# Third mixer's tiles: the transposed inverse by VectorE's 32x32 transposes, and another deal of the background pieces

## Chip, cores, metric

One core of a Trainium2 chip runs the whole program as one launch. The metric is the device time in microseconds, the median of three runs. All data is float32. TensorE takes the big products as three products of a high part and a remainder.

## The reference, cut to what matters

One layer of a hybrid decoder: RMSNorm, one input projection, four token mixers in parallel (HGRN2, RWKV-7, GLA, mLSTM), merge gates, an output projection, and an MLP with squared ReLU. 1040 prompt tokens (16 learned, 1024 given) and 8 sequences of 4 sample tokens share the weights. The change touches the RWKV-7 mixer, called here the third mixer, since the kernel runs it third. For each of its 4 heads (64 keys, 64 values), token by token:

```python
sa = jnp.einsum('bhvk,bhk->bhv', s, kkt)
s = (s * jnp.exp(lwt)[:, :, None, :] - sa[..., None] * (kkt * at)[:, :, None, :]
     + vt[..., None] * kt[:, :, None, :])
return s, jnp.einsum('bhvk,bhk->bhv', s, rt)
```

## The kernel before, in words

**Tiles.** The 1072 tokens are columns, padded to three groups of 358. The mixers run one after another: mLSTM, then HGRN2 and GLA together (the second mixer's loop), then RWKV-7. Each takes tiles of 128 tokens, 8 of them, and a ninth of 48 tokens, in which the last prompt tokens and the samples stand and masks keep the sequences apart. Within a tile RWKV-7's recurrence is solved in closed form: a strictly triangular 128x128 matrix A per head, of scores between the tokens' removal keys, gives the triangular inverse of (I - A), by which the right-hand side is multiplied; state and output follow.

**The inverse.** It is built by doubling. Level 0 puts the scores next to the diagonal into an identity matrix (blocks of 2). Level l, for l = 1 to 6 with halves of 2, 4, ... 64, joins pairs of blocks: it takes A times the first halves of the inverse, then the second halves' inverse times that. Two copies are kept, T in tile RTT (`tt`) and its transpose in RTI (`ti`), because a product on TensorE takes one operand transposed. The four heads stand side by side in 512 columns. A level is:

1. TensorE, L1226: four products of 64 columns (eight instructions in the trace) of A with `ti`, into a bank. They wait for `ti` of the level before.
2. ScalarE, L1644: copies them to RM1 (`m1`).
3. TensorE, L1234: `m1` with `tt`, which gives the new part of `ti` (not at the last level), and L1238: the same two the other way round, which gives the new part of `tt`.
4. VectorE, L2306 in `select`: puts the new part into `ti`, then into `tt`, under a mask, each after its product.

Besides, each tile has on TensorE at its head the scores (L1216 to L1218; L1218 gives those for `ti`), after level 1 the transposes of the output of the tile before (L1181), after level 2 the transposes of keys and values (L1246, L1248), after level 4 the right-hand side (L1200, L1192), the same lines again after level 6 for the output, the solution (L1259), the output (L1266) and the new state (L1284, L1285). VectorE masks the scores (`masked`, L2280), selects level 0 into `ti` (L2275) and into `tt` (L2287), and updates the state (L2354, L2359), for which the next tile's head waits (semaphore rw_pre).

**Background pieces.** While the mixers wait for other engines, TensorE works at the input projection of what comes later (here the merge gates). `fill_work` is a generator; one `steps(gate, k)` puts k pieces into TensorE's program at that place. A piece is three products of 358 columns (L442). Eight pieces fill one of two banks, 48 make one pair of weight chunks, and each pair of tiles consumes 48, so 24 to a tile. ScalarE empties the banks (`steps(outs, 1)`, three times a tile, one of them after level 4) and takes the high part of the next weights; GpSimd subtracts it to get the remainder.

**Order.** It is written out by hand. Each engine runs its own program in order and meets the others by counting semaphores. `rw_t` counts VectorE's results in a tile, `rw_n` the products of L1234 and L1238 that are ready, `rw_m` and `rw_m1` those of L1226 and the copies. `rw_ti`, `rw_tt` and the constants RW_PER_T, RW_PER_N say which count belongs to which level. The loop over tiles is a hardware loop over pairs, with the first pair and the ninth tile written apart. No planner is involved.

Of the kernel before, what the change touches and what calls it, by code (L numbers as in the profile page):

```python
# [26 lines left out]
HALVES = [1, 2, 4, 8, 16, 32, 64]  # L27
LHALVES = [1, 2, 4, 8]
# [109 lines left out]
def build(nc, A, OUT, fcols, ucols, fdim, udim):  # L138
    ctx = ExitStack()
    with ctx:  # L140
# [12 lines left out]
        def S(name):  # L153
            return sems[name]
# [12 lines left out]
        def PS(b, lo=0, hi=512):  # L167
            return PSt[:, b * 512 + lo:b * 512 + hi]
# [21 lines left out]
        def mask8(name, k, rows=P):  # L190
            o, n = ucols[name]
            w = {"lv": P, "lvt": P, "ll": LASTW, "llt": LASTW}[name]
            return CU[0:rows, o + k * w:o + (k + 1) * w]
# [33 lines left out]
        def half(x, h, second):  # L227

            names = " ".join("abc"[:len(x.shape) - 2])
            y = x.rearrange(f"p {names} (n t) -> p {names} n t", t=2 * h)  # L230
            return y[(slice(None),) * (len(y.shape) - 1) + (slice(h, 2 * h) if second else slice(0, h),)]
# [4 lines left out]
        def bc(x, shape):  # L236
            return x.to_broadcast(shape)
# [278 lines left out]
        def steps(work, k):  # L516
            for _ in range(k):
                next(work, None)
# [93 lines left out]
        Q_GL, Q_RW, Q_GATE, Q_END = 2, 7, 11, 27  # L612
        Q_GL_TILES, Q_GL_TAIL, Q_RW_PRE, Q_RW_TILES, Q_RW_TAIL = 9, 17, 18, 21, 25

        def rw_ti(l):
            return 1 if l == 0 else 3 if l == 1 else 2 * l + 2

        def rw_tt(l, last):
            return 2 if l == 0 else 4 if l == 1 else 2 * l + 2 if last else 2 * l + 3
        RW_PK, RW_PER_T, RW_PER_N = 5, 2 * len(HALVES), 2 * len(HALVES) - 3  # L620

# [293 lines left out]
        def _(e):  # L917
# [5 lines left out]
            for k in range(KD):  # L923
                e.wait_ge(S("ht_ready"), k + 1)
                for g in range(3):
                    last = e.matmul(PS(3 + g, 0, GRP)[0:68], WS[:, k, :], XT[:, k, g * GRP:(g + 1) * GRP],  # L926
                                    start=k == 0, stop=k == KD - 1)
# [3 lines left out]
                for g in range(3):  # L931
                    last = three(e, PS(g, 0, GRP), 0, k, slice(g * GRP, (g + 1) * GRP), k == 0, k == KD - 1)
# [12 lines left out]
            for t in range(TILES + 1):  # L945
                w = P if t < TILES else LASTW
                for u in range(2):
                    o = t * 2 * P + u * P
                    last = e.transpose(PSt[0:w, o:o + P], VT[:, u, t * P:t * P + w], ident)
# [4 lines left out]
            for q, src in enumerate((RSC, RKH)):  # L954
                for g in range(3):
                    last = e.matmul(PS(3 * q + g, 0, GRP), const("sel4", 4), src[:, g * GRP:(g + 1) * GRP],
                                    start=True, stop=True)
            last.then_inc(S("ml_bc"), 1)
            for t in range(TILES + 1):
                w = P if t < TILES else LASTW  # L960
                last = e.transpose(PS(0, GRP, 512)[0:w, 4 * t:4 * t + 4], RM[:, t * P:t * P + w], ident[0:4, 0:4])
# [67 lines left out]
            for g in range(3):  # L1029
                last = e.matmul(PS(g, 0, GRP), WGA[0:16, :], GA[0:16, g * GRP:(g + 1) * GRP], start=True, stop=True)  # L1030
# [139 lines left out]
            def rw_tile(n, w, last_tile, gate, rc, first=False):  # L1170
                levels = LHALVES if last_tile else HALVES
                nlev = len(levels)
# [39 lines left out]
                for h in range(4):  # L1212
                    r, g = slice(64 * (h % 2), 64 * (h % 2) + 64), h // 2

                    ab = rc[r, g:g + 3:2, 0:w]
                    e.matmul(PS(h % 2, g * 2 * w, (g + 1) * 2 * w)[0:w], rc[r, 6 + g, 0:w], ab, start=True, stop=True)  # L1216
                    e.matmul(PS(2 + h % 2, g * 2 * w, (g + 1) * 2 * w)[0:w], rc[r, 4 + g, 0:w], ab, start=True, stop=True)
                    last = e.matmul(PS(4 + h % 2, g * w, g * w + w)[0:w], rc[r, g, 0:w], rc[r, 6 + g, 0:w], start=True, stop=True)  # L1218
                last.then_inc(S("rw_s"), 1)
                steps(gate, 8 if last_tile else 7)  # L1220
                for l in range(1, nlev):

                    lh, m = levels[l], w // 2
                    e.wait_ge(S("rw_t"), t0 + (2 if l == 1 else rw_ti(l - 1)))
                    for h in range(4):
                        last = e.matmul(PS(4, h * m, h * m + m)[0:w], pb[0:w, 2 * h * w:2 * h * w + w],  # L1226
                                        half(ti[0:w, h * w:h * w + w], lh, False), start=True, stop=True)
                    last.then_inc(S("rw_m"), 1)
                    steps(gate, 6 if last_tile else 1)
                    e.wait_ge(S("rw_m1"), n * 6 + l)  # L1230
                    e.wait_ge(S("rw_t"), t0 + rw_tt(l - 1, False))
                    if l < nlev - 1:
                        for h in range(4):
                            last = e.matmul(PS(1, h * m, h * m + m)[0:w], tt[0:w, h * w:h * w + w],  # L1234
                                            half(m1[0:w, h * w:h * w + w], lh, False), start=True, stop=True)
                        last.then_inc(S("rw_n"), 1)
                    for h in range(4):
                        last = e.matmul(PS(0, h * m, h * m + m)[0:w], m1[0:w, h * w:h * w + w],  # L1238
                                        half(tt[0:w, h * w:h * w + w], lh, True), start=True, stop=True)
                    last.then_inc(S("rw_n"), 1)  # L1240
                    if l == 1 and not first:
                        back_to_rows(n - 1, P)
                    if l == 2:
                        e.wait_ge(S("rw_t"), t0 + RW_PK)
                        for j in range(4):
                            e.transpose(PS(2, j * P, j * P + P)[0:w], rc[:, 4 + j, 0:w], ident)  # L1246
                        for j in range(2):
                            last = e.transpose(PS(3, j * P, j * P + P)[0:w], rc[:, 8 + j, 0:w], ident)  # L1248
                        last.then_inc(S("rw_kt"), 1)
                    if l == 4:  # L1250
                        rhs()
# [2 lines left out]
                keys(1, 1)  # L1254
                seen(1, 1, False)
                e.wait_ge(S("rw_r"), n + 1)
                e.wait_ge(S("rw_t"), t0 + rw_tt(nlev - 1, True))
                for h in range(4):
                    last = e.matmul(PS(5, h * 64, h * 64 + 64)[0:w], tt[0:w, h * w:h * w + w], RRS[0:w, h * 64:h * 64 + 64],  # L1259
                                    start=True, stop=True)  # L1260
# [21 lines left out]
                else:  # L1282
# [2 lines left out]
                        last = e.matmul(PS(0, g * P, g * P + P), RKB[:, 256 + g * P:256 + g * P + P], RUS[:, g * P:g * P + P],  # L1285
                                        start=False, stop=True)
                    last.then_inc(S("rw_ds"), 1)
                steps(gate, 24 if last_tile else 9)
                if last_tile:
                    back_to_rows(n, w)  # L1290

# [472 lines left out]
        def _(e):  # L1764
# [3 lines left out]
            for i in range(KD // 2):  # L1768
                e.wait_ge(S("norm_sq"), 2 * i + 2)
                j = (2 * i) % 4  # L1770
# [457 lines left out]
            def rw_tile(n, w, last_tile, first=False):  # L2228
# [27 lines left out]
                if not last_tile:  # L2256
# [2 lines left out]
                        ec = REC[:, g, bass.ds(n, 1)]  # L2259
                        ins = e.tensor_scalar(RXC[:, g * P:g * P + P], RST0[:, g * P:g * P + P], ec, None, ALU.mult)  # L2260
                    st.did(ins)
                e.tensor_copy(ti, bc(idw.unsqueeze(1), [w, 4, w]))
                st.did(e.tensor_copy(tt, bc(idw.unsqueeze(1), [w, 4, w])))
                if not first:
                    r = [RMS_[:, k] for k in range(4)]
# [5 lines left out]

                mk = bc(mask8("ll" if last_tile else "lv", 0, w).unsqueeze(1), [w, 2, w])
                mkt = bc(mask8("llt" if last_tile else "lvt", 0, w).unsqueeze(1), [w, 2, w])
                for j in range(2):
                    ins = e.copy_predicated(ti[:, j:4:2, :], mkt, PS(4 + j, 0, 2 * w)[0:w].rearrange("p (h t) -> p h t", h=2))  # L2275
                ins.then_inc(S("rw_t"), 1)
                def masked(dst, bank):
                    for j in range(2):
                        out = dst.rearrange("p (i j c) -> p i j c", i=2, j=2)[:, :, j, :]
                        ins = e.tensor_tensor(out, PS(bank + j, 0, 4 * w)[0:w].rearrange("p (i c) -> p i c", i=2),  # L2280
                                              bc(cm.unsqueeze(1), [w, 2, 2 * w]), ALU.mult)
                    return ins
                masked(pb, 0)

                for j in range(2):
                    src = PS(j, 0, 4 * w)[0:w].rearrange("p (i k t) -> p i k t", i=2, k=2)[:, :, 0, :]
                    ins = e.copy_predicated(tt[:, j:4:2, :], mk, src)  # L2287
                ins.then_inc(S("rw_t"), 1)
                if last_tile:
                    e.wait_ge(S("states_in"), (11 + 8 + 4) * 16)  # L2290
                    e.wait_ge(S("rw_pre"), n + 1)
# [10 lines left out]
                def select(dst, bank, mk, ready):  # L2302
                    e.wait_ge(S("rw_t"), t0 + at)
                    e.wait_ge(S("rw_n"), n0 + ready)
                    e.sem_inc(S("select_turn"), 1)
                    e.copy_predicated(dst, bc(mk.unsqueeze(1), dst.shape),  # L2306
                                      PS(bank, 0, 2 * w)[0:w].rearrange("p (a n t) -> p a n t", a=4, t=h)).then_inc(S("rw_t"), 1)
                for l, h in list(enumerate(levels))[1:]:
                    if l < nlev - 1:
                        select(half(ti, h, False), 1, half(mask8("llt" if last_tile else "lvt", l, w), h, False), 2 * l - 1)  # L2310
                        at += 1
                    select(half(tt, h, True), 0, half(mask8("ll" if last_tile else "lv", l, w), h, True), 2 * l - (l == nlev - 1))
                    at += 1
                    if l == 1:
                        masked(pk, 2).then_inc(S("rw_t"), 1)
                        at += 1
                        if not first:
                            output(n - 1, P)
# [274 lines left out]
```

## Time and profile before

| | |
|---|---|
| median of 3 runs | 2424.34 us (2422.03 to 2425.43) |
| profiled execution | 2420.86 us, its span 2419.1 us |
| mean granted clock of TensorE | 0.958 |
| TensorE busy | 2215.7 us (92%) |
| VectorE busy | 1046.7 us (43%) |
| ScalarE busy | 609.4 us (25%) |
| GpSimd busy | 457.2 us (19%) |
| the 8 full tiles of the third mixer | from some 967 to 1275 us |

The span is the time from the first to the last instruction. PE is TensorE, PEld its loading of weights, which overlaps products, DVE VectorE, ACT ScalarE, POOL GpSimd, SP SyncE. L1226 is line 1226 of the kernel. PEclk is the granted clock of TensorE, 1.00 for 2.4 GHz and 0.50 for 1.2 GHz. In a timeline, "x8" are eight instructions merged, the time is from the first start to the last end, and the brackets give idle time before it and what ended it. The chain is followed back from the last instruction, and its pieces begin where the piece before ended. Ends of products are modelled.

### The profile page before, as it was taken

What the parts mean: (1) busy time and instruction counts of PE and PEld (TensorE: products, weight loads), DVE (VectorE), ACT (ScalarE), POOL (GpSimd) and SP (SyncE); (2) the same over time, 40 slices, a digit from 0 to 9 for tenths busy, and PEclk for the clock granted to TensorE, in tenths of its full rate; (3) what the DMA queues carried; (4) which work ended last, traced back from release to release, by engine and by line L of the source; (5) the groups of instructions that cost most, each with busy time, mean ns of one, the idle gap of its engine ahead of it and who ended that gap; (6) DMA issues with size and microseconds to landing.
All of it is one profiled execution on the core that took longest, in us unless ns stands there. A gap on an engine that the chain in (4) does not pass through costs nothing.

```text
span 2419.1 us, 33549 instructions
## 1 busy us (share of the span) xinstructions
PE 2215.7 (92%) x13459; PEld 2094.0 (87%) x13459; DVE 1046.7 (43%) x1568; ACT 609.4 (25%) x801; POOL 457.2 (19%) x463
## 2 busy tenths in 40 slices
PE   5989998899999888999998699999999979999995
PEld 3978787799899776999998689999999979999994
DVE  4142331565655545333333266642222225655554
ACT  3422221432322143212121143011000013333342
POOL 1131113344443421010000266110000010000012
PEclk9999998999999888999998799999999989999997
DMA  4121124222222231010101465131111233111112
GB/s 149 44 68 54 53 62 123 95 62 67 70 71 69 83 127 54 19 46 18 36 18 36 142 225 194 44 113 47 43 43 43 80 121 140 41 37 43 43 43 81
DMA packets 48562, 178.39 MB, mean 74 GB/s; under 512 B 6400, under 2 KB 6752, under 8 KB 48240
## 3 DMA queue, kind: packets, MB, share of 16 engines
q1 hardware_dynamic: 23040, 85.72, 11.7%
q0 software_dynamic: 17648, 62.03, 7.4%
q10 hardware_dynamic: 7808, 29.71, 3.2%
q8 instruction: 48, 0.79, 0.1%
q14 instruction: 18, 0.15, 0.0%
HBM read 129.41 MB, written 48.02 MB: 73 GB/s over the span
## 4 chain that ended last, share of the span: by engine, by line
PE 80%; DVE 6%; ACT 4%; issue 3%; DMA 3%; PEld 1%; POOL 1%; PEldq 0%; DVEq 0%; POOLq 0%; SPq 0%; ACTq 0%
PE PS L442 23%; PE PS L599 20%; PE PS L1355 15%; PE PS L1316 4%; PE PS L1059 2%; PE PS L1238 2%; PE PS L1234 2%; PE PS L1226 2%; DMA RING<-in_w_all 1%; PE PS L1071 1%; PEld PS L442 1%; PE PS L1192 1%; PE PS L926 1%; DVE AR L1979 1%; PE PS L1200 1%
## 5 line engine op out<-in xcount | busy, mean ns | idle before, releaser
L442 PE MATMUL PS<-HT_parts,WHIA_parts 128*128 128x358 f32 x1440 | 516.6, 359 | 37.1 <-POOL RING_parts L437 18.6
L442 PE MATMUL PS<-OT_parts,WHIA_parts 128*128 128x358 f32 x1440 | 482.1, 335 | 0.0
L442 PE MATMUL PS<-HT_parts,RING_parts 128*128 128x358 f32 x1440 | 480.1, 333 | 0.0
L1355 PE MATMUL PS<-ACT_parts,CF_parts 128*128 128x358 f32 x1152 | 319.0, 331 | 24.6 <-DVE ACT_parts L577 13.8
L442 PEld LDWEIGHTS PS<-HT_parts,WHIA_parts 128*128 128x128 f32 x1440 | 281.5, 195 | 58.1 <-POOL RING_parts L437 20.3
L437 POOL TENSOR_TENSOR RING_parts<-RING,WHIA_parts 128x1024 fp32r<-128x1024 f32 x60 | 154.0, 2566 | 856.3 <-ACT WHIA_parts L432 856.3
L442 PEld LDWEIGHTS PS<-OT_parts,WHIA_parts 128*128 128x128 f32 x1440 | 281.6, 196 | 3.6
L442 PEld LDWEIGHTS PS<-HT_parts,RING_parts 128*128 128x128 f32 x1440 | 280.6, 195 | 0.0
L599 PE MATMUL PS<-HT_parts,CF_parts 128*128 128x358 f32 x768 | 251.7, 328 | 0.9 <-ACT AR L566 0.9
L599 PE MATMUL PS<-OT_parts,CF_parts 128*128 128x358 f32 x768 | 251.2, 327 | 0.0
L599 PE MATMUL PS<-HT_parts,RING_parts 128*128 128x358 f32 x768 | 250.8, 327 | 0.0
L1355 PE MATMUL PS<-ACT_parts,RING_parts 128*128 128x358 f32 x768 | 250.3, 326 | 0.0
L1355 PEld LDWEIGHTS PS<-ACT_parts,CF_parts 128*128 128x128 f32 x1152 | 206.9, 189 | 33.9 <-issue 28.4
L1733 ACT ACTIVATE ACT_parts<-AR 128x1074 fp32r<-128x1074 f32 x96 | 105.8, 1103 | 192.9 <-PE PS L1355 178.5
L599 PEld LDWEIGHTS PS<-HT_parts,CF_parts 128*128 128x128 f32 x768 | 144.6, 188 | 1.3 <-ACT AR L566 1.2
L599 PEld LDWEIGHTS PS<-OT_parts,CF_parts 128*128 128x128 f32 x768 | 145.2, 189 | 0.1
L599 PEld LDWEIGHTS PS<-HT_parts,RING_parts 128*128 128x128 f32 x768 | 144.9, 189 | 0.0
L1355 PEld LDWEIGHTS PS<-ACT_parts,RING_parts 128*128 128x128 f32 x768 | 144.6, 188 | 0.0
L477 ACT ACTIVATE AR<-PS 128x358 f32<-128x358 f32 x102 | 47.6, 467 | 348.9 <-PE PS L442 348.8
L2444 DVE SCALAR_TENSOR_TENSOR AR<-PS,AR 128x1074 f32 (+1 forms) x32 | 40.8, 1276 | 208.5 <-PE PS L599 201.9
L1355 PE MATMUL PS<-CF_parts 128*128 128x358 f32 x384 | 125.2, 326 | 0.0
L551 POOL TENSOR_TENSOR AR<-AR 128x1074 f32<-128x1074 f32 x14 | 33.9, 2423 | 460.4 <-ACT AR L544 460.4
(392 smaller groups left out, 3523.7 us busy)
## 6 DMA issues: line engine op xcount, KB each, us to landing
RING<-in_w_all SPq DMA_DIRECT2D x132, 512.0 KB, 3.3
AR<-gates POOLq DMA_DIRECT2D x32, 537.0 KB, 4.0
proj<-AR ACTq DMA_DIRECT2D x18, 537.0 KB, 5.1
AR<-proj POOLq DMA_DIRECT2D x18, 537.0 KB, 8.6
gates<-CF ACTq DMA_DIRECT2D x16, 537.0 KB, 5.2
gates<-AR ACTq DMA_DIRECT2D x16, 537.0 KB, 5.3
AR<-in_xT SPq DMA_DIRECT2D x8, 537.0 KB, 14.4
AR<-in_xT POOLq DMA_DIRECT2D x8, 537.0 KB, 6.8
```

The costliest lines, as they stand in the source:

```text
L437: e.tensor_tensor(RING_R[:, u], RING[:, u], WHIA_R[:, u].bitcast(F32), ALU.subtract).then_inc(S(f"split{u}"), 1)
L442: last = e.matmul(out, a_[:, u, k, :], b_[:, k, t], start=first and i == 0, stop=end and i == 2)
L477: e.activation(row[:, g * GRP:(g + 1) * GRP], PS(6 + c % 2, 0, GRP), ACT.Copy).then_inc(S("fill_free"), 1)
L599: last = e.matmul(PS(3 * u + g, 0, GRP), a_[:, u, k, :], b_[:, k, t], start=k == 0 and i == 0, stop=k == KD - 1 and i == 2)
L1059: last = e.matmul(PS(3 * (l % 2), lo * m, hi * m)[0:w], x[:, g, l, 0:w], GQB[:, l % 2, lo * m:hi * m], start=True, stop=True)
L1226: last = e.matmul(PS(4, h * m, h * m + m)[0:w], pb[0:w, 2 * h * w:2 * h * w + w], half(ti[0:w, h * w:h * w + w], lh, False), start=True, s ...
L1234: last = e.matmul(PS(1, h * m, h * m + m)[0:w], tt[0:w, h * w:h * w + w], half(m1[0:w, h * w:h * w + w], lh, False), start=True, stop=True)
L1238: last = e.matmul(PS(0, h * m, h * m + m)[0:w], m1[0:w, h * w:h * w + w], half(tt[0:w, h * w:h * w + w], lh, True), start=True, stop=True)
L1316: last = e.matmul(PS(3 * u + tg, 0, GRP), a_[:, v, k, :], b_[:, k, t], start=k == 2 * br and i == 0, stop=k == 2 * br + 1 and i == 2)
L1355: last = e.matmul(PS(3 * v + g, 0, GRP), a_[:, u, 4 * v + r % 4, :], b_[b][:, t], start=r == 0 and i == 0, stop=r == 31 and i == 2)
L1733: e.activation(AHI_R[r % 2], act_row(r), ACT.Copy).then_inc(S("act_hi"), 1)
L2444: e.scalar_tensor_tensor(row3(dst), cols3(3 * u), 0.0, row3(RST2), ALU.max, ALU.mult).then_inc(S(f"banks_free{u}"), 1)
```

## The change

In the eight full tiles `ti` is no longer built by products up to level 4, that is up to blocks of 32. VectorE transposes all of `tt` in 32x32 blocks into `ti` (`flip`, 128x512 elements in one instruction) at level 0 and after the select of `tt` at levels 1 to 4. Since `tt` then holds nothing outside its blocks of 32, this is its transpose. L1218, L1234 of levels 1 to 4, L2262, L2275 and the selects into `ti` of levels 1 to 4 go. At levels 5 and 6, and in the ninth tile, all stays. VectorE now selects level 0 into `tt` before the masking, and the transpose stands behind it. L1226 waits for the transpose of the level before. The counts are renumbered. The pieces of a tile are dealt out otherwise: 5 after the scores (7 before), 3 between L1226 and the next product at levels 1 to 4 (1 before), 1 at levels 5 and 6 as before, 2 after L1259 as before, 3 at the end (9 before).

```diff
-                    last = e.matmul(PS(4 + h % 2, g * w, g * w + w)[0:w], rc[r, g, 0:w], rc[r, 6 + g, 0:w], start=True, stop=True)
+                    if last_tile:
+                        last = e.matmul(PS(4 + h % 2, g * w, g * w + w)[0:w], rc[r, g, 0:w], rc[r, 6 + g, 0:w], start=True, stop=True)
                 last.then_inc(S("rw_s"), 1)
-                steps(gate, 8 if last_tile else 7)
+                steps(gate, 8 if last_tile else 5)
...
-                    steps(gate, 6 if last_tile else 1)
+                    steps(gate, 6 if last_tile else 3 if l <= RW_FLIPS else 1)
                     e.wait_ge(S("rw_m1"), n * 6 + l)
-                    e.wait_ge(S("rw_t"), t0 + rw_tt(l - 1, False))
-                    if l < nlev - 1:
+                    e.wait_ge(S("rw_t"), t0 + rw_tt(l - 1, last_tile))
+                    if l < nlev - 1 and (last_tile or l > RW_FLIPS):
...
-                steps(gate, 24 if last_tile else 9)
+                steps(gate, 24 if last_tile else 3)
...
+                def flip(at):
+
+                    e.wait_ge(S("rw_t"), t0 + at)
+                    e.transpose(flat[0], flat[1]).then_inc(S("rw_t"), 1)
+                if last_tile:
+                    masked(pb, 0)
+                    first_level()
+                else:
+                    first_level()
+                    masked(pb, 0)
+                    flip(1)
...
+                    flips = not last_tile and l <= RW_FLIPS
+                    if l < nlev - 1 and not flips:
+                        select(half(ti, h, False), 1, half(mask8("llt" if last_tile else "lvt", l, w), h, False), rw_n(l, last_tile, False))
                         at += 1
...
+                    if flips:
+                        flip(at)
+                        at += 1
```

## Rows read from the trace of the kernel before

**Rows 1.** Page, chain that ended last: share of the span by engine.
```profile
PE 80%; DVE 6%; ACT 4%; issue 3%; DMA 3%; PEld 1%; POOL 1%; PEldq 0%; DVEq 0%; POOLq 0%; SPq 0%; ACTq 0%
```

**Rows 2.** Stretches of one third-mixer tile: engines' busy us, granted clock, DMA.
```profile
core 0: us, PE busy (x) PEld busy (x) DVE busy (x) ACT busy (x) POOL busy (x), PEclk, DMA share, GB/s
...
1044.70:1082.99 38.29, 37.90 (x288) 35.67 (x289) 13.96 (x36) 7.95 (x19) 2.36 (x1) 1.00 0.10 29
```

**Rows 3.** Chain in that tile, in order of time: start us, us, what.
```profile
1044.72 0.67 PE PS L1216 x2
...
1047.66 3.65 PE PS L442 x21
...
1052.16 0.55 PE PS L442 x3
1052.71 1.05 PE PS L1234 x8
1053.75 0.89 PE PS L1238 x8
1054.65 0.22 PE PS L1181 x2
...
1058.34 0.44 PE PS L1246 x4
1058.79 0.22 PE PS L1248 x2
...
1061.49 0.89 PE PS L1238 x8
1062.38 0.89 PE PS L1226 x8
...
1065.83 0.89 PE PS L1200 x8
1066.72 0.50 PE PS L1192 x4
...
1078.20 4.44 PE PS L442 x27
```

**Rows 4.** Groups of VectorE's instructions, 880 to 1300 us: busy us, mean ns.
```profile
L2280 DVE TENSOR_TENSOR AR<-PS,CF 128x512 f32<-128x512 f32 x32 | 20.6, 686 | 0.0
...
L2158 DVE SCALAR_TENSOR_TENSOR AR<-AR,CC 128x1039 f32<-128x1039 f32 x4 | 5.2, 1293 | 0.0
...
L2263 DVE COPY AR<-CF 128x512 f32<-128x512 f32 x8 | 3.3, 419 | 0.0
```

**Rows 5.** VectorE in that tile, in order of time: start us, us, instruction.
```profile
1047.92 0.78 DVE L2275 COPY_PREDICATED AR<-CU,PS 128x256 f32<-128x256 uint8 x2 [4.94 <-PE PS L1218]
...
1049.79 0.77 DVE L2287 COPY_PREDICATED AR<-CU,PS 128x256 f32<-128x256 uint8 x2
...
1054.87 0.73 DVE L2306 COPY_PREDICATED AR<-CU,PS 128x256 f32<-128x256 uint8 x1 [0.23 <-PE PS L1238]
...
1062.54 0.43 DVE L2306 COPY_PREDICATED AR<-CU,PS 128x256 f32<-128x256 uint8 x1 [0.46 <-PE PS L1238]
...
1079.04 0.61 DVE L2359 SCALAR_TENSOR_TENSOR AR<-AR 128x128 f32<-128x128 f32 x2
```

**Rows 6.** TensorE in that tile, in order of time.
```profile
1062.22 1.06 PE L1226 MATMUL PS<-AR 128*128 128x64 f32 x8
```

**Rows 7.** Stretches with and without the full clock, columns as in rows 2.
```profile
487.14:527.46 40.32, 39.41 (x243) 37.32 (x242) 23.04 (x53) 10.81 (x17) 16.30 (x24) 0.96 0.20 59
527.46:566.34 38.88, 37.97 (x243) 35.76 (x242) 23.17 (x53) 10.72 (x17) 17.43 (x24) 1.00 0.20 62
...
909.54:911.83 2.29, 0.33 (x2) 0.03 (x1) 2.29 (x3) 0.00 (x0) 0.00 (x0) 1.00 0.00 0
...
913.20:926.80 13.60, 13.49 (x34) 9.56 (x33) 3.20 (x3) 5.59 (x5) 0.00 (x0) 0.50 0.00 1
1312.60:1336.40 23.80, 20.84 (x88) 20.33 (x89) 10.04 (x27) 1.42 (x2) 1.08 (x1) 0.50 0.00 1
```

More of the change, by code:

```diff
@@ L613, in build, with rw_ti, rw_tt, rw_n @@
         Q_GL_TILES, Q_GL_TAIL, Q_RW_PRE, Q_RW_TILES, Q_RW_TAIL = 9, 17, 18, 21, 25
[L615 to L620, printed above, removed]
+        def rw_ti(l, last_tile):
+            if last_tile:
+                return 1 if l == 0 else 3 if l == 1 else 2 * l + 2
+            return 2 if l == 0 else 4 if l == 1 else 2 * l + 3 if l <= RW_FLIPS else 2 * l + 2
+        def rw_tt(l, last_tile):
+            nlev = len(LHALVES if last_tile else HALVES)
+            if last_tile:
+                return 2 if l == 0 else 4 if l == 1 else 2 * l + 2 if l == nlev - 1 else 2 * l + 3
+            return 1 if l == 0 else 3 if l == 1 else 2 * l + 2 if l <= RW_FLIPS or l == nlev - 1 else 2 * l + 3
+        def rw_n(l, last_tile, second):
+            flips = 0 if last_tile else RW_FLIPS
+            if l <= flips:
+                return l
+            nlev = len(LHALVES if last_tile else HALVES)
+            return flips + 2 * (l - flips) - (1 if l == nlev - 1 or not second else 0)
+        RW_FLIPS = 4
+        RW_PK, RW_PER_T, RW_PER_N = 5, 2 * len(HALVES), 2 * len(HALVES) - 3 - RW_FLIPS
         @block.sync
@@ L1216, in rw_tile @@
                     e.matmul(PS(h % 2, g * 2 * w, (g + 1) * 2 * w)[0:w], rc[r, 6 + g, 0:w], ab, start=True, stop=True)
-                    e.matmul(PS(2 + h % 2, g * 2 * w, (g + 1) * 2 * w)[0:w], rc[r, 4 + g, 0:w], ab, start=True, stop=True)
-                    last = e.matmul(PS(4 + h % 2, g * w, g * w + w)[0:w], rc[r, g, 0:w], rc[r, 6 + g, 0:w], start=True, stop=True)
+                    last = e.matmul(PS(2 + h % 2, g * 2 * w, (g + 1) * 2 * w)[0:w], rc[r, 4 + g, 0:w], ab, start=True, stop=True)
+                    if last_tile:
+                        last = e.matmul(PS(4 + h % 2, g * w, g * w + w)[0:w], rc[r, g, 0:w], rc[r, 6 + g, 0:w], start=True, stop=True)
                 last.then_inc(S("rw_s"), 1)
-                steps(gate, 8 if last_tile else 7)
+                steps(gate, 8 if last_tile else 5)
                 for l in range(1, nlev):
                     lh, m = levels[l], w // 2
-                    e.wait_ge(S("rw_t"), t0 + (2 if l == 1 else rw_ti(l - 1)))
+                    e.wait_ge(S("rw_t"), t0 + (2 if l == 1 else rw_ti(l - 1, last_tile)))
                     for h in range(4):
@@ L1256, in rw_tile @@
                 e.wait_ge(S("rw_r"), n + 1)
-                e.wait_ge(S("rw_t"), t0 + rw_tt(nlev - 1, True))
+                e.wait_ge(S("rw_t"), t0 + rw_tt(nlev - 1, last_tile))
                 for h in range(4):
@@ L2261, in rw_tile @@
                     st.did(ins)
-                e.tensor_copy(ti, bc(idw.unsqueeze(1), [w, 4, w]))
+                if last_tile:
+                    e.tensor_copy(ti, bc(idw.unsqueeze(1), [w, 4, w]))
                 st.did(e.tensor_copy(tt, bc(idw.unsqueeze(1), [w, 4, w])))
@@ L2273, in rw_tile @@
                 mkt = bc(mask8("llt" if last_tile else "lvt", 0, w).unsqueeze(1), [w, 2, w])
-                for j in range(2):
-                    ins = e.copy_predicated(ti[:, j:4:2, :], mkt, PS(4 + j, 0, 2 * w)[0:w].rearrange("p (h t) -> p h t", h=2))
-                ins.then_inc(S("rw_t"), 1)
+                if last_tile:
+                    for j in range(2):
+                        ins = e.copy_predicated(ti[:, j:4:2, :], mkt, PS(4 + j, 0, 2 * w)[0:w].rearrange("p (h t) -> p h t", h=2))
+                    ins.then_inc(S("rw_t"), 1)
                 def masked(dst, bank):
@@ L2282, in masked, with first_level @@
                     return ins
[L2283 to L2288, printed above, removed]
+                def first_level():
+                    for j in range(2):
+                        src = PS(j, 0, 4 * w)[0:w].rearrange("p (i k t) -> p i k t", i=2, k=2)[:, :, 0, :]
+                        ins = e.copy_predicated(tt[:, j:4:2, :], mk, src)
+                    ins.then_inc(S("rw_t"), 1)
+                def flip(at):
+                    e.wait_ge(S("rw_t"), t0 + at)
+                    e.transpose(flat[0], flat[1]).then_inc(S("rw_t"), 1)
+                if last_tile:
+                    masked(pb, 0)
[4 more added lines that the diff above has]
+                    flip(1)
                 if last_tile:
@@ L2308, in rw_tile @@
                 for l, h in list(enumerate(levels))[1:]:
-                    if l < nlev - 1:
-                        select(half(ti, h, False), 1, half(mask8("llt" if last_tile else "lvt", l, w), h, False), 2 * l - 1)
+                    flips = not last_tile and l <= RW_FLIPS
+                    if l < nlev - 1 and not flips:
+                        select(half(ti, h, False), 1, half(mask8("llt" if last_tile else "lvt", l, w), h, False), rw_n(l, last_tile, False))
                         at += 1
-                    select(half(tt, h, True), 0, half(mask8("ll" if last_tile else "lv", l, w), h, True), 2 * l - (l == nlev - 1))
+                    select(half(tt, h, True), 0, half(mask8("ll" if last_tile else "lv", l, w), h, True), rw_n(l, last_tile, True))
                     at += 1
+                    if flips:
+                        flip(at)
+                        at += 1
                     if l == 1:
```

## The prediction

> **What bounds the kernel now.** The chain that ended last is read first: TensorE products hold 80% of it [rows 1]. Then the table of stretches, one row for each third-mixer tile: the tile from 1044.70 to 1082.99 us lasts 38.29 us, TensorE shows work for 37.90 of them and its granted clock is 1.00, its upper level, 2.4 GHz [rows 2]. VectorE is busy for 13.96 us and ScalarE for 7.95 us. Last the chain inside that tile, in order of time [rows 3]: products follow each other without a hole, because each wait for VectorE is covered by products that TensorE still has to issue, and each wait for ScalarE by one piece of the background projection. So what is taken from TensorE's list in these tiles is a gain, as long as it does not uncover a wait. There are 8 such tiles; the short ninth keeps its old way.
>
> **What the change removes from TensorE.** Each number is for one tile.
> - L1218, the transposed first-level scores: 8 of the 24 passes that run from 1044.72 to 1047.66 [rows 3]. 2.94 / 24 = 0.12 us each, so 0.98 us.
> - L1234, the product for the transposed inverse, at levels 1 to 4. Before, one piece (0.55 us) and L1234 (1.05 us, part of it waiting for ScalarE's copy) stand between L1226 and L1238, together 1.60 us at level 1; the other three levels repeat this at 1.64 to 1.65 [rows 3]. The piece is kept, at 0.52 (21 matmuls, seven pieces, in 3.65 us [rows 3]). So 1.08 + 1.13 + 1.12 + 1.13 = 4.46 us go. That the copy stays hidden follows: three pieces, 1.56 us, now stand where 0.55 us of piece and a short wait stood.
> Removed: 5.44 us. The 24 pieces per tile are only dealt out anew (5 + 4x3 + 2x1 + 2 + 3 in place of 7 + 6x1 + 2 + 9), so they cost the same.
>
> **What it adds.** The transposed block is now a copy of the block that L1238 has just given: select, then a transpose of 128x512 elements on VectorE (call its time F), then the next L1226. Between L1238 and that L1226 TensorE has no piece: all three stand after L1226. Before, L1234's result was selected while L1238 ran, which hid it. TensorE issues in order, so the pieces behind L1226 wait too.
>
> The trace before has no transpose on VectorE. The nearest rows are 0.42 us for a plain copy of 128x512 (L2263), 0.69 us for a product of 128x512 with a PSUM source (L2280) and 1.29 us for 128x1039 (L2158), as if each element went through twice [rows 4]. I take 0.69: the same number of elements, and the copy's faster pace needs no reordering across lanes. The ends are kept for the range. No gain below zero is possible: the transpose is a new instruction in a chain of dependent ones.
>
> At level 3, L1238 ends at 62.38; the select runs from 62.54 for 0.43 [rows 5], to 62.97; the transpose to 63.66; 0.15 for the wake-up (as L1238 to select) gives 63.81. TensorE would have gone on at 62.38, and L1226 also loses an overlap of 0.17 with its predecessor (1.06 alone [rows 6] against 0.89 in the chain [rows 3]). Stall: 1.43 + 0.17 = 1.60 us. The other levels differ by what TensorE still has behind L1238:
> - level 1: the select takes 0.73 from 54.87 [rows 5], so 55.60 + 0.69 + 0.15 = 56.44, against 54.87 when L1181 ends: 1.57 + 0.17 = 1.74.
> - level 2: L1246 and L1248 cover 0.66: 0.94.
> - level 4: L1200 and L1192 cover 1.39: 0.21.
> Sum over levels: 1.74 + 0.94 + 1.60 + 0.21 = 4.49 us.
>
> At the head five pieces end at 47.66 + 2.60 = 50.26. VectorE's two selects and two masks take until about 49.79, as before but in the other order [rows 5]; with the transpose and the wake-up 50.63: 0.37 + 0.17 = 0.54. At the tail three pieces, 3 x 0.49 (27 in 4.44 [rows 3]), end at 79.68; the state update L2359 ends at 79.65 [rows 5], plus 0.15 = 79.80: 0.12 + 0.17 = 0.29. Nine pieces covered it before. The copy L2262 (0.42, as L2263 [rows 4]) and the two selects L2275 (0.78) that leave VectorE free it before the next tile, where it waits anyway: nothing. Behind the transpose of level 1 VectorE has the masked key products (2 x 0.69 [rows 4]) and the output of the tile before; level 2's three pieces and two products (1.56 + 2 x 0.89) run meanwhile, so they are covered. The background bank's evacuation by ScalarE falls due earlier in the tile, two pieces after the copy of level 4 behind which it is issued; ScalarE is busy for a fifth of the tile [rows 2], so nothing is put down. Without that cover TensorE would wait some tenths once a tile, 0.8 us in all for each tenth.
>
> Added: 4.49 + 0.54 + 0.29 = 5.32 us. Net at an unchanged clock: 5.32 - 5.44 = -0.12 us a tile, -1 us over 8. With F = 0.42 each of four transposes gives back 0.27 and level 4 its 0.21: -10 us more, so -11. With F = 1.29 five grow by 0.60: +24, so +23.
>
> A rule bears on F. By the Trainium skill, "VectorE: DVE Perf Modes", section "The three transpose paths", the engine transposes 128x128 in bf16 in 311 ns; four times that, an estimate from the page without any fixed part shared, is 1.24 us, and the sum would be +21 us. No transpose in the rows can settle it.
>
> **The clock.** This term decides. Today these tiles stand at 1.00. The rows show where it falls [rows 7]. From 909.54 to 911.83 TensorE worked for only 0.33 us, and from 913.20 the clock was at 0.50, its lower level, 1.2 GHz, for 13.60 us. In a tile of the second mixer, the stretch from 487.14, a drop came with TensorE busy for 39.41 of 40.32 us: the mean is 0.96, and the next tile, with the same work, stays at 1.00. And it doesn't come back by being busy: from 1312.60 to 1336.40 TensorE was busy for 20.84 of 23.80 us, mostly with the ninth tile's thin state products, and stayed at 0.50. The new tile puts, twice (after levels 1 and 3), products of 64 columns for 0.9 us, a hole of 1.4 to 1.6 us, and again 0.9 us of them, with no piece between. The hole is a little shorter than the one at 909.54; the work on both sides of it is thinner than a piece, whose products have 358 columns. The level 2 and level 4 places are filled by transposes and right sides.
>
> Price: the tile at 0.96 takes 40.32 against 38.88, 1.44 us more, and 0.04 x 2 x 40.32 = 3.2 us of it were at half: 0.45 us for each us at half. How often and for how long is an estimate. Of 16 such places I let 6 drop the clock, in six different tiles: of the two tiles of the second mixer one fell. A low stretch lasts between 3.2 (second mixer) and 23.8 us; 11 is taken, since the five pieces of the next head are the first solid work after level 4. 6 x 11 x 0.45 = 30 us. Bounds: 0, and 8 x 23.8 x 0.45 = 86 us.
>
> The same is said by the Trainium skill, "TensorE: Matmul & The Clock Gate", section "A second HAM failure mode: psum-queue depth-cycling": short idles between groups of products make the clock swing between its two rates. It speaks against this change, and the rows agree with it.
>
> **Sum.** -1 + 30 = +29 us. The profiled execution took 2420.86 us (span 2419.1 and 1.8 around it), 3.5 below the median of the runs, 2424.34. From the median: 2453 us. Faster or slower means by over 0.2%, 4.9 us, about what a measurement tells from no change.
>
> **Rivals.**
> - The clock holds and the transposes are short. Place: the hole behind L1238, levels 1 and 3. Price: F = 0.42 gives -11 us, 2413. For it: before, 24 thin products a level at 1.00 with one piece never cost the clock, and each hole is under 2 us. Against: those had no hole at all. It decides below F of about 0.6, if the clock stays at 1.00.
> - The clock holds, F near 0.69: the products go and as long waits come, 2423. For it: every step's size is read from rows. Against: the clock rows.
> - The clock falls in every tile and stays low until the next head: 8 x 20 x 0.45 = 72 us, 2495. For it: the stretch to 1336.40. Against: three pieces a level are solid work in between.
> - Transposes go at the slow pace with the clock holding: +23, 2447.
>
> **Chances.** Forecast (the clock falls in some tiles) 0.52, all tiles 0.12, slow transposes with the clock holding 0.05, clock holds and no change 0.18, clock holds and short transposes 0.13. Of the first, few falls may leave it near zero. So slower 0.68, same 0.18, faster 0.14. Range 2417 to 2488: from the clock-holds cases to most of the every-tile case; the forecast alone, two to eleven drops at 5 us each, has 2433 to 2478.
>
> **What would show it.** The tile's stretch in the table: clock below 1.00 in several of the eight, lengths unequal, some near 38 us and some over 42. TensorE idle behind L1238 at levels 1 and 3 by 1.4 to 1.6 us, at level 4 under 0.3, released by VectorE's transpose; a transpose row near 0.69 us. L1234 at a third of its count, L1218 only in the ninth tile. It is wrong if all eight stand at 1.00, or if TensorE's holes are under 1 us.

## Result and profile after

The changed kernel takes 2436.82 us (median of 6 runs, 2429.98 to 2450.85) against 2423.40 for the kernel before beside it (6 runs, 2422.03 to 2425.46): 13.4 us more, a ratio of 1.006 [1.0031, 1.0089]. A second series of 12 runs gave 1.0049 [1.0032, 1.0067]. It is slower, within the forecast's range, and by less than half of what was forecast. The profiled execution took 2435.24 us (span 2433.7) at a mean granted clock of 0.954, where the one before took 2420.86 us at 0.958. L1226 is now L1240, L1234 is L1248, L1238 is L1252, L1181 is L1194, L1200 is L1213, L1259 is L1273, L2306 is L2334, and the new transpose is L2309.

The page's chain by engine is that of [rows 1] within a per cent; it doesn't tell the two kernels apart.

```profile
PE 81%; DVE 6%; ACT 4%; issue 3%; DMA 3%; POOL 1%; PEldq 0%; POOLq 0%; DVEq 0%; PEld 0%; SPq 0%; ACTq 0%
```

The stretches do. Each row is one third-mixer tile of the changed kernel, and the last lies inside one; columns as in rows 2.

```profile
1008.32:1049.01 40.69, 36.64 (x249) 34.46 (x249) 14.44 (x34) 8.06 (x19) 7.10 (x6) 0.92 0.12 40
1049.01:1089.54 40.53, 36.79 (x249) 34.48 (x249) 14.64 (x35) 7.87 (x19) 2.35 (x1) 0.92 0.08 28
1089.54:1127.77 38.23, 33.74 (x249) 31.33 (x249) 14.91 (x37) 8.31 (x20) 2.36 (x1) 1.00 0.08 29
...
1061.20:1064.50 3.30, 3.30 (x17) 3.30 (x16) 0.71 (x3) 0.00 (x0) 0.00 (x0) 0.50 0.00 0
```

TensorE has 40 matmuls fewer in a tile than in [rows 2] (249 for 289, by the count of weight loads: L1218 and four levels of L1248), and in the tile with the full clock it works 33.74 us in place of 37.90. That tile is hardly shorter than before all the same (38.23 us; the same tile took 38.66). The tiles ahead of it stand at 0.92 and last 2.3 to 2.5 us longer, with the same work. The last row lies in one of the drops, as stretches at half clock are called here: the clock is at its lower level, 1.2 GHz, and TensorE is busy throughout. All eight tiles, from head to head:

| tile | 0 | 1 | 2 | 3 | 4 | 5 | 6 | 7 | sum |
|---|---|---|---|---|---|---|---|---|---|
| before, us | 39.94 | 38.03 | 38.27 | 38.66 | 38.26 | 38.65 | 38.26 | 38.40 | 308.5 |
| after, us | 40.86 | 40.69 | 40.53 | 38.23 | 40.73 | 40.90 | 37.83 | 40.88 | 320.6 |
| us at half clock, before | 4.4 | 0 | 0 | 0 | 0 | 0 | 0 | 0 | 4.4 |
| us at half clock, after | 8.3 | 6.8 | 6.8 | 0 | 6.8 | 6.8 | 0 | 6.8 | 42.3 |

So 12.2 of the 14.6 us between the two spans lie in these tiles. Of the other 2.4 us, 0.7 lie ahead of the first tile's head and 1.7 behind the eighth tile; they were not followed to a line.

What fills a tile that keeps the clock is seen in its chain of waits (start us, us, what), the tile from 1089.54, level 1 and the start of level 2. It answers to [rows 3].

```profile
1093.82 0.63 DVE AR L2309
...
1094.49 1.10 PE PS L1240 x8
1095.59 1.54 PE PS L442 x9
1097.14 0.85 PE PS L1252 x8
...
1098.12 0.73 DVE AR L2334
...
1098.88 0.72 DVE AR L2309
...
1099.65 1.10 PE PS L1240 x8
```

L1248 is gone from levels 1 to 4. The three pieces stand where one piece and L1234 stood, and behind L1252 the chain passes over to VectorE, to the select and the transpose, before the next level can start. TensorE's own order shows these waits in brackets: idle time before a group, here called a hole, and what ended it, at levels 2 and 4 (behind L1252 of levels 1 and 3).

```profile
1099.65 1.10 PE L1240 MATMUL PS<-AR 128*128 128x64 f32 x8 [1.45 <-DVE AR L2309]
...
1109.36 1.10 PE L1240 MATMUL PS<-AR 128*128 128x64 f32 x8 [1.37 <-DVE AR L2309]
```

VectorE's group for the transpose, over the stage (columns as in rows 4), gives its price:

```profile
L2309 DVE STREAM_TRANSPOSE AR<-AR 128x512 f32<-128x512 f32 x40 | 28.4, 710 | 1.1
```

The chain in the tile from 1049.01, behind its second drop, shows where the clock goes back up:

```profile
1070.03 1.10 PE PS L1240 x8
1071.13 2.51 PE PS L442 x9
1073.64 1.43 PE PS L1252 x8
1075.07 0.89 PE PS L1213 x8
```

The drop begins at 1071.3, with level 4's three pieces, which take 2.51 us where 1.54 is their time at the full clock. It ends at 1074.7, within L1252, and the next group is back at 0.89, as at the full clock. All 11 new drops of this execution last 3.4 us, two in each of five tiles and one in the first, each behind a hole of 1.4 us.

### The profile page after: what moved, and what is told of

The parts are those of the page before. It is cut to its first block, busy times and chain, and to the rows that moved or that the text cites. A ratio compares the mean times of both kernels' runs of the same rounds, so it can differ in the third digit from the quotient of the medians.

```text
span 2433.7 us, 32840 instructions
## 1 busy us (share of the span) xinstructions
PE 2192.4 (90%) x13139; PEld 2071.3 (85%) x13139; DVE 1049.5 (43%) x1552; ACT 609.0 (25%) x801; POOL 469.5 (19%) x463
## 4 chain that ended last, share of the span: by engine, by line
PE 81%; DVE 6%; ACT 4%; issue 3%; DMA 3%; POOL 1%; PEldq 0%; POOLq 0%; DVEq 0%; PEld 0%; SPq 0%; ACTq 0%
PE PS L442 25%; PE PS L599 19%; PE PS L1369 15%; PE PS L1330 4%; PE PS L1240 2%; PE PS L1072 2%; PE PS L1252 2%; DVE AR L2309 1%; PE PS L1084 1%; DMA RING<-in_w_all 1%; PE PS L939 1%; PE PS L1205 1%; PE PS L1107 1%; PE PS L1213 1%; PE PS L1100 1%
## 5 line engine op out<-in xcount | busy, mean ns | idle before, releaser
L437 POOL TENSOR_TENSOR RING_parts<-RING,WHIA_parts 128x1024 fp32r<-128x1024 f32 x60 | 163.0, 2716 | 870.8 <-ACT WHIA_parts L432 870.8
```

Source lines behind the costliest of these rows:

```text
L437: e.tensor_tensor(RING_R[:, u], RING[:, u], WHIA_R[:, u].bitcast(F32), ALU.subtract).then_inc(S(f"split{u}"), 1)
```

## Experiments

In what follows thin products are those of 64 columns, solid ones the pieces' of 358, and the deal is how a tile's 24 pieces are spread over it. Theory 1: the products removed and the waits added weigh about the same, and the slowdown is the clock, which falls at the holes behind L1252. Theory 2: the waits alone do it, and the clock's drops are small beside them. The ratios are against the kernel before, run on the same chip in turn: 2425.56 us for the first four kernels, 2427.27 for the next four, 2427.64 for the last two.

**Discarded products in the holes.** Ten products of 256 columns, whose result is never read, stand behind L1252 of levels 1 and 3. They fill most of the holes of 1.4 us (0.27 and 0.15 us are left, still ended by the transpose) and take nothing away.

```diff
+                    if not last_tile and l in (1, 3):
+                        for _ in range(10):
+                            e.matmul(PS(4, 256, 512), HT_R[:, 0, 0:P], HT_R[:, 0, 0:256], start=True, stop=True)
```

> The change, and ten products of 256 columns (some 1.2 us, their result is never read) behind L1252 at levels 1 and 3 of each full tile, shorter than the holes there (1.4 to 1.6 us), so that no wait gets longer. Theory 1, the clock: the change loses 2.7 us in each of six tiles because the clock drops for 3.4 us twice in them, and drops because those two holes leave TensorE too little to do. Then all eight tiles stand at 1.00 and take 37.8 to 38.3 us, and the whole is 16 us under the change: 2420 us, 0.998 of before. Theory 2, the waits: the holes themselves cost the time and the clock is a bystander. Then filling them with useless work brings nothing: 2437, or later.

Measured: 2421.22 us (2416.11 to 2427.16), ratio 0.9993 [0.9981, 1.0004]. One tile's stretch (columns as in rows 2); the other tiles are like it, the first at 0.95 as before the change:

```profile
1083.70:1121.91 38.21, 36.12 (x268) 33.70 (x269) 14.94 (x37) 8.30 (x20) 2.35 (x1) 1.00 0.08 29
```

TensorE works 2.4 us more than in the tile of 38.23 us above (36.12 against 33.74), in the same length, and the kernel takes 0.9993 of the time before where the changed one takes 1.006. Theory 2 falls: with the same waits for VectorE the kernel takes no longer than the kernel before, once TensorE works through them. Theory 1 holds.

**Pieces behind L1252.** The same holes, filled with work that is needed: level 1 and 3 have one piece behind L1240 and three behind L1252, levels 2 and 4 one and one.

```diff
-                    steps(gate, 6 if last_tile else 3 if l <= RW_FLIPS else 1)
+                    steps(gate, 6 if last_tile else {1: 1, 2: 1, 3: 1, 4: 1}.get(l, 1))
...
+                    if not last_tile:
+                        steps(gate, {1: 3, 2: 1, 3: 3, 4: 1}.get(l, 0))
```

> The change with its pieces in another place: behind L1226 one piece at each level, and behind L1252 (the product whose result is transposed) 3, 1, 3, 1 at levels 1 to 4; head 5, tail 3, as in the change. Theory 1: the holes are filled by useful work, so the clock stays at 1.00 and the wait for the transpose is hidden; by the rows of before, 38.3 less 5.4 removed, plus 0.6 (the wait for ScalarE's copy is back), 0.85 left of the holes and 0.8 at head and tail = 35.2 us a tile, 25 us under before: 2398, 0.990. Theory 2 (the chain of VectorE sets the tile, wherever the pieces stand): 38 us a tile, 2420 to 2437.

Measured: 2400.74 us (2398.18 to 2410.57), ratio 0.99 [0.9884, 0.9917]; tiles of 34.86 to 35.52 us at 1.00, but for the first (36.45 us at 0.93). A tile, and the chain at level 1 (in the tile before it):

```profile
1085.97:1121.49 35.52, 34.36 (x248) 31.05 (x249) 14.94 (x37) 8.28 (x20) 2.35 (x1) 1.00 0.09 31
```

```profile
1057.43 1.10 PE PS L1252 x8
1058.53 1.53 PE PS L442 x9
1060.07 0.22 PE PS L1194 x2
1060.28 1.04 PE PS L1240 x8
```

From L1252 to the next L1240 the chain stays on TensorE: VectorE's select and transpose are hidden under the pieces. A tile is 3.1 us shorter than before (38.66 to 35.52 for the one shown), 25 us over eight. So the transposes do bring a gain when the pieces stand behind the products that they wait for.

**The old deal with the transposes.** 7 pieces at the head, 1 a level, 9 at the tail, all else as changed.

```diff
-                steps(gate, 8 if last_tile else 5)
+                steps(gate, 8 if last_tile else 7)
...
-                    steps(gate, 6 if last_tile else 3 if l <= RW_FLIPS else 1)
+                    steps(gate, 6 if last_tile else 1)
...
-                steps(gate, 24 if last_tile else 3)
+                steps(gate, 24 if last_tile else 9)
```

> The change with the pieces dealt as before (7 at the head, 1 a level, 9 at the end): the transposes alone. Theory 1: the same holes with two pieces less a level around them, so the clock drops more often and stays down longer, 10 to 20 us a tile: 2450 to 2480 us. Theory 2 (the loss comes from the new deal, that is from the waits it uncovers at head and tail): those waits are covered again, 4.7 removed against 4.5 of holes a tile: 2421 us, the clock aside.

Measured: 2542.15 us (2527.49 to 2555.85), ratio 1.0483 [1.0465, 1.05]. The direction is theory 1's; the size is missed by 60 us, since I had each drop last too short. A tile, and the chain of waits in the tile before it:

```profile
1085.56:1140.11 54.55, 51.26 (x248) 49.49 (x249) 14.61 (x34) 8.06 (x19) 2.36 (x1) 0.62 0.07 20
```

```profile
1040.76 1.97 PE PS L1240 x8
1042.73 1.00 PE PS L442 x3
1043.73 1.61 PE PS L1252 x8
...
1079.69 5.41 PE PS L442 x27
```

Its tiles last 54.4 to 55.0 us, but for the first of 56.70 and one of 47.18. 41 us of the 54.55 are at half clock (0.38 x 2 x 54.55), and each group takes up to twice its time (L1252 1.61 against 0.85, a piece 1.00 against 0.52). One piece a level doesn't bring the clock back; it rises in the nine pieces of the tail, but in the tile of 47.18 us already in the two pieces behind L1273. Against the 38.39 us of the same tile with the clock held (the old deal with discarded products, below) that is 16.2 us for 41 us at half clock, 0.40 for each.

**The new deal without the transposes.** The kernel before with 5, 3 a level up to level 4, and 3.

```diff
-                steps(gate, 8 if last_tile else 7)
+                steps(gate, 8 if last_tile else 5)
...
-                    steps(gate, 6 if last_tile else 1)
+                    steps(gate, 6 if last_tile else 3 if l <= 4 else 1)
...
-                steps(gate, 24 if last_tile else 9)
+                steps(gate, 24 if last_tile else 3)
```

> The kernel before with only the new deal of the pieces (5, 3 at levels 1 to 4, 1 at levels 5 and 6, 2, 3), no transposes. Theory 1: no hole arises, the clock stays at 1.00 in all tiles; the wait for ScalarE's copy goes (0.6 us a tile) and waits at head and tail come (0.8): within 4 us of before, 2419 to 2427. Theory 2 (the deal itself costs, by ScalarE's evacuations falling due too early or by the tail's cover): 10 us or more over before, 2433.

Measured: 2420.23 us (2416.24 to 2427.64), ratio 0.9985 [0.997, 1.0]. A tile:

```profile
1082.39:1120.62 38.23, 37.20 (x289) 35.67 (x289) 14.41 (x39) 8.28 (x20) 2.35 (x1) 1.00 0.08 29
```

The deal alone doesn't lower the clock: no hole over 0.3 us stands among its thin products. The two parts of the change don't add. The deal alone is worth about -4 us (its interval -7 to 0), the transposes alone +117, both together +13: the deal is what keeps the transposes' drops short.

**Discarded products at level 1 only, and at level 3 only.** Which of the two holes costs?

```diff
-                    if not last_tile and l in (1, 3):
+                    if not last_tile and l in (1,):
```

> The change with the ten discarded products behind L1252 at level 1 alone; the hole of level 3 stays open. Theory 1a, each hole drops the clock by itself: one drop of 3.4 us stays in most tiles, 1.35 us each, so some 8 us over the run with both holes filled (2421): 2428 to 2431 us. Theory 1b, the first drop brings on the second (the tile is late and thin after it): with level 1 filled both go, and the time is that of the run with both filled, 2421 us.

Measured: 2446.24 us (2438.76 to 2452.59), ratio 1.0077 [1.0051, 1.0103]. Both expectations were below it. There were fewer drops (three new ones in the profiled execution), but one of them lasted 27.3 us. Its tile and the one behind it, and the chain from level 4 to the next head:

```profile
1053.89:1103.73 49.84, 46.92 (x258) 45.31 (x259) 15.68 (x38) 8.66 (x21) 2.35 (x1) 0.73 0.07 23
1103.73:1141.95 38.22, 34.88 (x259) 32.53 (x259) 13.98 (x34) 7.64 (x18) 2.35 (x1) 1.00 0.10 29
```

```profile
1074.83 2.10 PE PS L442 x9
1076.92 1.60 PE PS L1252 x8
1078.52 1.71 PE PS L1213 x8
...
1082.79 1.00 PE PS L442 x3
...
1095.67 1.90 PE PS L442 x6
...
1100.98 2.40 PE PS L442 x9
```

The clock fell at 1075.6, when part of level 4's pieces had already gone. What was left of them didn't bring it back, nor did the single pieces of levels 5 and 6 (1.00) and the two behind the solution (1.90); it rose in the three of the tail, after 27.3 us. Two pieces at that place are not always too few: in the old deal's tile of 47.18 us the clock rose in them, after 20.5 us, and the next group is back at 0.84.

```profile
1343.35 1.66 PE PS L442 x6
1345.01 0.84 PE PS L1280 x8
```

The same hole, then, costs 1.4 us (3.4 x 0.40) or 11.6 (49.84 - 38.22), by how much solid work is still to come behind the fall, and when. That is a reading of where the drops ended; no run here varied the moment of the fall by itself.

The other one:

```diff
-                    if not last_tile and l in (1, 3):
+                    if not last_tile and l in (3,):
```

> The mirror image: the ten discarded products behind L1252 at level 3 alone; the hole of level 1 stays open. With level 1 filled (2446 us) fewer tiles dropped, but one drop, behind level 3, lasted 27 us: after level 4 there is no solid work before the next head. Theory: what a drop costs depends on the pieces that follow it. A drop at level 1 is followed by three levels of three pieces, so each lasts 3.4 us (some 6.8): up to 1.4 us in each of eight tiles, on the 2421 of both holes filled: 2422 to 2433 us, no stretch over 10 us. Rival: the length is a matter of chance or of the hole's size alone (level 1's is the longer one): as with level 1 filled, 2440 or more.

Measured: 2426.75 us (2423.22 to 2430.34), ratio 0.9997 [0.9987, 1.0007]. In the profiled execution a single tile dropped once, for 3.4 us:

```profile
1163.82:1203.46 39.64, 36.52 (x259) 34.06 (x259) 14.88 (x37) 8.30 (x20) 2.36 (x1) 0.96 0.08 27
```

So the hole behind level 3 is the costly one, and with it filled the one behind level 1, open in all eight tiles, is nearly harmless. Why it drops the clock in one tile here and in five of the changed kernel is not shown.

**Old deal with discarded products.** The 2542 us kernel with the ten products at levels 1 and 3.

```diff
+                    if not last_tile and l in (1, 3):
+                        for _ in range(10):
+                            e.matmul(PS(4, 256, 512), HT_R[:, 0, 0:P], HT_R[:, 0, 0:256], start=True, stop=True)
```

> The transposes with the old deal of the pieces (7, 1 a level, 9), which took 2542 us with its tiles at half clock for 41 of 54.6 us, and in it the ten discarded products behind L1252 at levels 1 and 3. Theory 1: more work on TensorE makes it faster by some 120 us: the clock stays at 1.00 for most of the tile, 37.5 to 38.5 us a tile, 2416 to 2424 us. Theory 2 (the old deal loses by its waits): as slow as without them, 2542, or slower by the 20 us that the products take.

Measured: 2426.68 us (2417.30 to 2430.44), ratio 0.9993 [0.9977, 1.0009]. A tile:

```profile
1090.43:1129.20 38.77, 36.84 (x269) 33.64 (x269) 14.56 (x34) 8.21 (x19) 2.36 (x1) 1.00 0.09 29
```

The time is 2.7 us above the upper end of what was expected. All tiles but the first are at 1.00, and 160 useless products (20 in each of 8 tiles) save 115 us.

**Two pieces a level.** Between the old and the new deal: 6 at the head, 2 a level up to level 4, 6 at the tail.

```diff
-                steps(gate, 8 if last_tile else 5)
+                steps(gate, 8 if last_tile else 6)
...
-                    steps(gate, 6 if last_tile else 3 if l <= RW_FLIPS else 1)
+                    steps(gate, 6 if last_tile else 2 if l <= RW_FLIPS else 1)
...
-                steps(gate, 24 if last_tile else 3)
+                steps(gate, 24 if last_tile else 6)
```

> The change with two pieces behind L1226 at levels 1 to 4 in place of three (head 6, tail 6). It asks how long the clock stays down. Theory 1, it comes back when a level has enough solid work at half clock: three pieces gave 6.8 us low in a tile that dropped, one piece gave 41, so two lie between, 10 to 30 us a tile: 2450 to 2520 us. Rival: a drop lasts 3.4 us whatever the deal and the 41 us of the old deal come from its long thin stretch behind level 4: then about 2437 us as the change.

Measured: 2470.55 us (2462.09 to 2485.12), ratio 1.0179 [1.0127, 1.023]. Two tiles that follow each other:

```profile
1110.19:1161.68 51.49, 47.82 (x249) 46.34 (x249) 14.52 (x34) 8.22 (x19) 2.35 (x1) 0.67 0.07 22
1161.68:1199.98 38.30, 34.95 (x248) 32.81 (x249) 14.51 (x34) 7.92 (x18) 2.35 (x1) 0.96 0.09 28
```

Its drops last 3.4, 20.5 or 34.1 us. One, two and three pieces a level with the same holes give +117, +43 and +13 us: the less solid work behind a hole, the longer the clock stays down. The head and the tail of a tile change along with it, since its pieces stay 24.

**Pieces behind L1252, dealt once more.** 6 at the head; 3, 2 and 3 behind L1252 of levels 1 to 3 and none at level 4, whose hole the right-hand side covers; ScalarE empties the bank a level earlier.

```diff
...
+                        steps(gate, {1: 3, 2: 2, 3: 3}.get(l, 0))
...
-                steps(gate, 4 if last_tile else 2)
+                steps(gate, 4 if last_tile else 1)
...
-                    if l == 4 or last_tile:
+                    if l == 3 or last_tile:
```

> The version with pieces behind L1252 (2401 us), dealt a little further: head 6, one piece behind L1226, 3, 2, 3, 0 behind L1252 at levels 1 to 4, one behind L1259; ScalarE empties the background bank after level 3 in place of 4, since its ninth piece falls due earlier. By its chain some 0.45 us is left open behind L1252 at level 2 and 0.3 at the head, while level 4 is covered by the right side anyway: 0.3 to 0.4 us less a tile, 2397 to 2399 us. Rival: the chain of VectorE and ScalarE, not the cover, sets 4.1 to 4.5 us a level there: 2401 or later.

Measured: 2396.20 us (2393.37 to 2404.23), ratio 0.9881 [0.9851, 0.9912]. A tile:

```profile
1072.93:1107.99 35.06, 34.29 (x249) 31.11 (x249) 14.92 (x37) 8.25 (x20) 2.36 (x1) 1.00 0.09 32
```

TensorE is idle for 0.8 us of it. This version is 1.2% faster than the kernel before (interval 0.9 to 1.5%). That it beats the other deal behind L1252 is not shown: the intervals overlap.

**The changed kernel once more.**

> The changed kernel again, beside it on the same chip, for how its time scatters. Theory of the clock: its runs follow their mean granted clock (0.001 of it is 0.001 x 2 x 2437 = 4.9 us at half clock, some 2 us at 0.4 each), median 2430 to 2445, and they scatter over 10 to 25 us where before scatters over less than 10. Rival, holes alone: as narrow as before.

Measured: 2437.29 us (2429.16 to 2447.27, 12 runs), ratio 1.0049 [1.0032, 1.0067]. Its time follows the mean granted clock of the execution, from 2429.19 us at 0.956 to 2447.04 at 0.948. By these two, 0.008 x 2 x 2437 = 39 us more at half clock cost 18 us, 0.46 for each. The changed kernel's runs spread over 18 us here, the 23 of the kernel before on the same chip over 10.

## Why the prediction was wrong in its size

**The bound, right.** TensorE's list sets the length of these tiles, and what leaves it is a gain only where no wait is uncovered. The version with pieces behind L1252 gives the gain alone, the change gives it back.

**What is removed, right.** 40 instructions a tile; level 1's chain from L1240 on is 1.10, 1.54 and 0.85, with no trace of ScalarE's copy, as said. L1218 was put a little high: the head's products end 2.09 us after its start, 0.85 less than the 2.94 before, not 0.98; its products have 128 columns, those beside it 256, and a third of the time was put down for it.

**The transpose, right.** 0.71 us, against the 0.69 taken from the nearest row [rows 4]. The 311 ns for 128x128 in bf16 that the Trainium skill gives in "VectorE: DVE Perf Modes", section "The three transpose paths", made an estimate of 1.24 us by four times the width; the measured row decides, and for this size and type it is shorter.

**The holes, right within 0.15 us each, but for the tail's.** Idle behind levels 1 to 4: 1.45, 0.71, 1.37 and none, against 1.57, 0.77, 1.43 and 0.04; at the head 0.22 for 0.37. At the tail 0.12 + 0.17 = 0.29 was put as added, and nothing came: the hole there, 0.35 and some 0.73 us in turn, is as long before the change, with nine pieces in the tail, as after it, with three. The same tile's head, before and after:

```profile
1082.99 0.67 PE L1216 MATMUL PS<-AR 64*128 64x256 f32 x2 [0.35 <-issue]
1089.54 0.71 PE L1229 MATMUL PS<-AR 64*128 64x256 f32 x4 [0.35 <-DVE AR L2391]
```

A tile at the full clock became 0.43 us shorter (38.66 to 38.23, 38.26 to 37.83) against 0.12 forecast: -3.4 us over 8, not -1. The kernel with discarded products stands for this case without the drops: -1.7 us by its ratio (interval -4.6 to +1.0).

**The clock, right in place and number of tiles.** Lengths unequal, two near 38 us, the clock below 1.00 in six tiles beyond what they had before, behind levels 1 and 3. That it is just six is luck in part: the number rested on one tile of two in the second mixer, and the profiled execution of the second series has seven. The trace agrees with the Trainium skill's "TensorE: Matmul & The Clock Gate", section "A second HAM failure mode: psum-queue depth-cycling", by which short idles between groups of products make the clock swing: 11 drops here, each behind a hole of 1.4 us. The lengths over 42 us that I named as a mark did not come: the longest is 40.90.

**The step that failed** is the length of a low stretch, "11 is taken, since the five pieces of the next head are the first solid work after level 4". The three pieces of level 2 and of level 4 stand right behind the two holes, and they end a drop after 3.4 us, the lower end of the range that I had read (3.2 to 23.8 [rows 7]). The chain behind 1071.13 shows it, and the runs with one and two pieces show what happens without it: 41 us, and up to 34. I had counted the pieces between levels against the every-tile rival and left them out of the length. The other terms: 11 drops in place of 6 (two in five tiles, one in another), and a price of 0.41 for 0.45. With a tile's 0.43 us taken off, the eight tiles are 12.2 + 3.4 = 15.6 us longer than they would be, for 42.3 - 4.4 = 37.9 us at half clock, 0.41 for each. So the term is 15.6 us where 6 x 11 x 0.45 = 30 was put. The low count hid part of the error in the length: six drops of 3.4 us would have made 8.

**The rivals.** Clock holds with short transposes (2413) and with long ones (2447): out by the 0.71 us. Clock holds, no change (2423): it is what the discarded products make. Falls that last to the next head (2495): not in this kernel, but, up to the pieces of the tail, in the old deal with the transposes, in nearly every tile, with two pieces a level in two tiles, and once in the kernel with products at level 1 only.

What stays open: why the same tile drops in one execution and not in the next (tiles 3 and 6 kept the clock, in the second series' profiled execution tile 3 alone), and why a hole of 1.66 us behind level 1 of the first tile dropped nothing.

## What to carry to other kernels

When a change trades TensorE products for a wait on another engine, look at what TensorE does in the wait and right behind it: put independent solid products behind the instruction whose result is awaited, not ahead of it. A hole of 1.4 us between thin products cost, besides its own length, a drop of the clock here, and how long the clock stayed low went with the solid work that followed; judge it by the granted clock of the stretch, not by TensorE's busy share, which rose when the clock fell (33.74 of 38.23 us at 1.00, 51.26 of 54.55 at 0.62).

## What was unexpected of the hardware

- Products whose result nobody reads made kernels faster: 2436.82 to 2421.22 us, and 2542.15 to 2426.68.
- Taking one of two holes away made the kernel no faster (2446.24): of its three drops one came with less solid work behind it and lasted 27.3 us.
- At half clock single pieces between thin products didn't bring the clock back for 41 us, with TensorE busy for 51.26 of a tile's 54.55 us.
